# Order of the 28 products of a pair of swiglu units: by chunk pair instead of by product

## Chip, cores and metric

The kernel runs on one NeuronCore of a Trainium2 chip, in one launch. The metric is the device time in microseconds (us). Before the change it is 2767.7 us, the median of three runs (2762.27, 2767.70 and 2773.89). Everything is float32.

## The reference

Two blocks follow each other on one sequence of 256 tokens and width 1024. The first is an attention and gating layer with a mixture of 16 experts. The second is two layers (DEPTH_2 = 2), each with a swiglu, a mixer of four branches and a second swiglu. The changed code belongs to the swiglus of the second block, four in all:

```
D_MODEL = 1024; D_FF = 2816; DEPTH_2 = 2
def swiglu(x, w_gate, w_up, w_down):
    return (jax.nn.silu(x @ w_gate) * (x @ w_up)) @ w_down
for l in range(DEPTH_2):
    x = x + 0.5 * swiglu(rms_norm(x, ffn1_norm[l]), ffn1_w_gate[l], ffn1_w_up[l], ffn1_w_down[l])
    ...                                   # mixer
    x = x + 0.5 * swiglu(rms_norm(x, ffn2_norm[l]), ffn2_w_gate[l], ffn2_w_up[l], ffn2_w_down[l])
```

## The kernel before

**Weights.** SyncE loads all weights in units of 128 x 2048 float32 (1 MB) into a ring of 12 slots. A unit's load waits until the unit 12 places earlier is done, which TensorE tells through the semaphore unit_done. A swiglu stage has 11 pairs (PAIRS) of a gate unit and an up unit, each 256 columns of w_gate and w_up. Then come 11 units of w_down for the steps.

**Products.** For a pair j, both [256 tokens x 1024] x [1024 x 256] products are made together with seven products of halves instead of eight (a Strassen-like scheme). Tokens are halved into rows 0 to 127 and 128 to 255, and the contraction is halved into even and odd 128-blocks. The contraction of 1024 is eight chunks, or four chunk pairs k = 0 to 3. Product i of chunk pair k is one 128x128 by 128x256 product, and the profile shows it as two matmul instructions. So a pair has 7 x 4 = 28 products, or 56 matmuls. Their operands are the chunks of ZT (products 1, 2, 4), sums of activation chunks (3, 5, 6, 7, written by input_sums), and units of the ring or sums of weights (4, 5, 6; 7 reads a half of the up unit that VectorE has overwritten with a difference). VectorE makes the weight sums of a pair in four operations (pair_weights, L2455 to L2461, two of them as part 0 and two as part 1). Each adds one to weights_summed. GpSimd makes those of the very first pair (L2985 to L2990).

**PSUM.** Two sets of four banks alternate between pairs. In a set, product 1 has bank 3. Products 2 and 6 share bank 0, 5 and 7 share bank 1, 3 and 4 share bank 2.

**TensorE's order.** It is written out by hand. ffn runs pair 0, then pairs 1 to 10, then 22 steps for w_down (L1278). In the function pair, all four chunk pairs of product 1 come first, then those of 2, 3, 6, 7, 5 and 4. Pair 0 of the first stage of layer 0 goes through pair; the other three pair 0s go through by_chunks (from L1341), which already runs over chunk pairs and, in each, over 1, 2, 3, 6, 7, 5, 4. Before product 5 of pair j, turn_hidden (L1309 and L1316) transposes the hidden rows of pair j-1. In pair 0 of the first stage the small gain sums of final_sums (L1249, 32 matmuls of two columns) stand there instead. At its start a pair j >= 2 waits for hidden_out of pair j-2, a pair 1 of the first stage waits ahead of product 3 for mean_ready, and product 6 and product 4 wait for three and four of the weight sums.

**Behind the products.** ScalarE copies product 1 (L1940) after the first ffn_full. VectorE adds banks 0, 1 and 2 in turn (combine, L2533, L2536, L2540 and L2541), each behind the product that fills the bank. ScalarE applies silu (L1954, L1956), VectorE multiplies (L2614) into the hidden rows H, and ScalarE copies the transposed rows out (L1969, hidden_out). In pairs 1 to 4 of the first stage ScalarE has two more copies in front of that (L1964). ScalarE's program order is: silu of j, silu of j, product 1 of j+1, turned rows of j. VectorE's is: combine of j, weight sums of j+2 part 0, H of j, weight sums of j+2 part 1.

**Ahead of the first stage.** The input chunks of ZT are made by ScalarE (L1895) and VectorE (L2360), the activation sums by VectorE (L2465 to L2470).

Of the kernel before, what the change touches and what calls it, by code (L numbers as in the profile page):

```python
# [125 lines left out]
def nth_summed(l, st, i):  # L126

    n = nth_weights(l, st)
    if i == 0 and (l, st) == (0, FFN1):
        return 0  # L130
    if i == 0 and st != PROJ:
        before = (l, PROJ) if st == FFN2 else (l - 1, FFN2)
        return nth_weights(*before) + NEXT_AT[before[1]]
    return n + i + (st in NEXT_AT and (l, st) != (NL - 1, FFN2) and i >= NEXT_AT[st])
# [82 lines left out]
def build(nc, a, out, const, const_at):  # L217
    with ExitStack() as ctx:
# [84 lines left out]
        unit_done = sem("unit_done")  # L303
# [90 lines left out]
        ffn_full = sem("ffn_full")  # L394
        weights_summed = sem("weights_summed")
        acts_summed = sem("acts_summed")
        sums_used = sem("sums_used")
# [460 lines left out]
        def _(pe):  # L858
# [48 lines left out]
            def zg_chunk(v, k):  # L907

                if by_scalar(v, k):
                    pe.wait_ge(zg_out_a, chunk_out(v, k))  # L910
                else:
                    pe.wait_ge(zg_out_v, chunk_out(v, k))
# [19 lines left out]
            for b in range(4):  # L932
                for c in range(2):
                    for t in range(TT):
                        last = tr(ps[:, b, 256 * c + P * t:256 * c + P * t + P],
                                  X[:, t, P * (2 * b + c):P * (2 * b + c) + P], ident)
# [12 lines left out]
            for m, u in enumerate((0, 1, 2, 2, 3, 4, 5, 6)):  # L949
# [4 lines left out]
                for t in range(TT):  # L954
                    for k in range(KC):
                        if m in (0, 3) and t == 0:
                            pe.wait_ge((lhs_a, lhs_v)[k % 2], 4 * (m // 3) + k // 2 + 1)
                        last = mm(ps[:, 4 + m % 4, 256 * t:256 * t + 256], src[:, k, P * t:P * t + P],
                                  slot(U_WIN + u)[:, 256 * k:256 * k + 256], start=(k == 0), stop=(k == KC - 1))
# [4 lines left out]
            for n in range(2):  # L964
                for g in range(4):
                    last = tr(ps[:, n, P * g:P * g + P], wsR[:, 4 * n + g, :], ident)
                last.then_inc(turn_full, 1)
            pe.wait_ge(heads_ready, 1)
            for n in range(2):
                for c in range(2):  # L970
                    for t in range(TT):
                        last = tr(ps[:, 2 + n, 256 * c + P * t:256 * c + P * t + P],
                                  RQ1[:, t, 2 * (2 * n + c):2 * (2 * n + c) + 2, :].rearrange("p h d -> p (h d)"), ident)
# [3 lines left out]
            for g in range(2):  # L977
                for s in range(4):
                    last = tr(ps[:, g, P * s:P * s + P], KN1[:, s, g].rearrange("p u d -> p (u d)"), ident)
# [80 lines left out]
            for t in range(TT):  # L1060
                for g in range(8):
                    last = mm(ps[:, t, HD * g:HD * g + HD], wsT[:, g, :], B1[:, t, FB_VV + HD * g:FB_VV + HD * g + HD],
                              start=True, stop=True)
# [15 lines left out]
            for k in range(KC):  # L1079
                last = mm(ps[:, 7, 16:16 + NE], BB[:, k, :], slot(U_ROUTER)[:, NE * k:NE * k + NE],  # L1080
                          start=(k == 0), stop=(k == KC - 1))
            for i in range(2):
                for h in range(2):
                    last = mm(ps[64 * h:64 * h + 64, 7, 32:40].rearrange("p (j i) -> p i j", i=2)[:, i, :],
                              ident.rearrange("p (q i) -> p i q", i=2)[:, i, :],
                              scaleB[:, 2, :].rearrange("p (j h) -> p h j", h=2)[:, h, :], start=True, stop=True)
# [6 lines left out]
            for c in range(KC):  # L1093
                if c >= 4:
                    pe.wait_ge(xt_new, c - 3)
                for k in range(KC):
                    if c == 0:
                        pe.wait_ge(y_out, k // 2 + 1)
                        if k % 2 == 0:
                            wait_unit(pe, U_WOUT + k // 2)  # L1100
                    last = mm(ps[:, 4 + c % 4, 256 * (c // 4):256 * (c // 4) + 256],
                              slot(U_WOUT + k // 2)[:, D * (k % 2) + P * c:D * (k % 2) + P * c + P], ZT[:, k, :],
                              start=(k == 0), stop=(k == KC - 1))
# [6 lines left out]
            for k in range(KC):  # L1110
# [4 lines left out]
                for t in range(TT):  # L1115
                    last = mm(ps[:, 4, NE * t:NE * t + NE], RZ[:, k, P * t:P * t + P], slot(U_ROUTER)[:, NE * k:NE * k + NE],
                              start=(k == 0 and t == 0), stop=(k == KC - 1), skip_group_check=True)
# [10 lines left out]
            for t in range(TT):  # L1128
                last = tr(ps[0:NE, 5, P * t:P * t + P], AFF[:, t, :], ident)
# [106 lines left out]
            for l in range(NL):  # L1236
# [7 lines left out]
                def final_sums():  # L1244

                    for t in range(TT):
                        for k in range(KC):
                            pe.wait_ge(squares_out, KC + k + 1)
                            last = mm(ps[:, 2, 2 * t:2 * t + 2], SQ0[:, k, P * t:P * t + P], gsq[:, k, :],  # L1249
                                      start=(k == 0), stop=(k == KC - 1))  # L1250
                    last.then_inc(sums_out, 1)
# [45 lines left out]
                def ffn(st, first, v):  # L1297
# [3 lines left out]
                    def turn_hidden(j):  # L1301

                        pe.wait_ge(ffn_hidden, done + j + 1)
                        at = 4 * pair_set(st, j)
                        if v == 1 and 1 <= j < 5:
                            pe.wait_ge(fin_scaled, 1)
                            for c in range(2):
                                for t in range(TT):
                                    tr(ps[:, at + 1, 256 * c + P * t:256 * c + P * t + P],  # L1309
                                       XT[:, 2 * (j - 1) + c, P * t:P * t + P], ident)  # L1310
                        if st == FFN2 and l + 1 < NL and j == 1:
                            pe.wait_ge(v2_in, 16 * V2_LOADS * (l + 2))
                            tr(ps[:, at + 1, 0:V2_N], vrow[0:V2_N, :], ident[0:V2_N, 0:V2_N]).then_inc(cols_turned, 1)
                        for e in range(2):
                            for t in range(TT):
                                last = tr(ps[:, at, 256 * e + P * t:256 * e + P * t + P], H[:, t, P * e:P * e + P], ident)  # L1316
                        last.then_inc(rows_turned, 1)

                    def product(j, i, k, **kw):

                        n = U_LAYER + first + 2 * j
                        gate, up = slot(n), slot(n + 1)
                        even, odd = slice(512 * k, 512 * k + 256), slice(512 * k + 256, 512 * k + 512)
                        sums, wsum = z_sums(k // 2)[:, k % 2], pair_sums(j)
                        at = product_out(pair_set(st, j), i)
                        if i == 1:
                            return mm(at, ZT[:, 2 * k, 0:P], gate[:, even], **kw)  # L1327
                        if i == 2:
                            return mm(at, ZT[:, 2 * k + 1, 0:P], gate[:, odd], **kw)  # L1329
                        if i == 3:  # L1330
                            return mm(at, sums[:, 3], up[:, odd], **kw)  # L1331
                        if i == 4:
                            return mm(at, ZT[:, 2 * k + 1, P:T], wsum[:, 2, k], **kw)  # L1333
                        if i == 5:
                            return mm(at, sums[:, 0], wsum[:, 0, k], **kw)  # L1335
                        if i == 6:
                            return mm(at, sums[:, 1], wsum[:, 1, k], **kw)  # L1337
                        return mm(at, sums[:, 2], up[:, even], **kw)  # L1338
# [28 lines left out]
                    def pair(j):  # L1367

                        wait_unit(pe, U_LAYER + first + 2 * j, turns)
                        wait_unit(pe, U_LAYER + first + 2 * j + 1, turns)  # L1370
                        if j >= 2:
                            pe.wait_ge(hidden_out, done + j - 1)
                        for i in (1, 2, 3, 6, 7, 5, 4):
                            if j == 1 and i == 3 and v == 1:
                                pe.wait_ge(mean_ready, 3)
                            if i == 6:
                                pe.wait_ge(weights_summed, 4 * nth_summed(l, st, j) + 3)
                            if i == 5 and j:
                                turn_hidden(j - 1)
                            if i == 5 and j == 0:  # L1380
                                final_sums()
                            if i == 4:
                                pe.wait_ge(weights_summed, 4 * nth_summed(l, st, j) + 4)
                            for k in range(4):
                                if j == 0 and i < 3:
                                    zg_chunk(v, 2 * k + i - 1)
                                if j == 0 and i == 3 and k % 2 == 0:
                                    pe.wait_ge(acts_summed, 4 * (ns + k // 2) + 4)
                                last = product(j, i, k, start=(k == 0), stop=(k == 3))
                                if i == 4 and k < 2:  # L1390
                                    last.then_inc(unit_done, 1)
                            if i in (1, 6, 5):
                                last.then_inc(ffn_full, 1)
                        last.then_inc(sums_used, 1)

                    def before(i, b, k):

# [153 lines left out]
                for s in range(2):  # L1551
                    for hh in range(2):
                        last = mm(ps[:, 4, 64 * s + 32 * hh:64 * s + 32 * hh + 30], GB[:, s, P * hh:P * hh + P], C("stack")[:, 0:30],
                                  start=True, stop=True)
# [1491 lines left out]
```

## Time and profile before

| | us or share |
|---|---|
| Median of three runs | 2767.7 |
| The profiled execution's own time | 2772.29 |
| Its span (first to last instruction) | 2770.5 |
| TensorE matmul busy | 2551.8 (92%) |
| VectorE busy | 991.1 (36%) |
| ScalarE busy | 430.9 (16%) |
| Mean granted TensorE clock | 0.917 |
| One pair in steady state | 12.53 |

The profile is of one execution, and all rows quoted below come from it. Times in its tables count from the start of the span. The first 1145 us are the first block. The four swiglu stages start at 1150, 1758, 1967 and 2558 us. The granted clock is given as a share of full speed: 1.00 is 2.4 GHz and 0.50 is 1.2 GHz. Matmuls overlap by a little, so the spacing of their starts, not their duration, is what one costs.

### The profile page before, as it was taken

The numbers are of one execution on the slowest core, as the hardware profiler recorded it, in microseconds if no ns is written. First come the engines' busy times: TensorE is split into PE (matmuls) and PEld (weight loads), VectorE is DVE, ScalarE is ACT, GpSimd is POOL, SyncE is SP. The second block draws the span as 40 slices with busy tenths as digits, with TensorE's granted clock in tenths as the row PEclk, the third lists the DMA queues.
The fourth block names the chain that finished last, engine by engine and source line by source line (L and its number), as shares of the span: only waits on it lengthen the run. The fifth ranks groups of instructions, "written<-read, shape, count | busy, mean of one in ns | idle before, by whom it ended". The sixth has DMA issues, their size and how long they took to land.

```text
span 2770.5 us, 33932 instructions
## 1 busy us (share of the span) xinstructions
PE 2551.8 (92%) x14163; PEld 1951.3 (70%) x14163; DVE 991.1 (36%) x2011; ACT 430.9 (16%) x960; POOL 57.1 (2%) x65
## 2 busy tenths in 40 slices
PE   7998878888888878799999999999999999999999
PEld 5784434444445444588898788888888897788888
DVE  1421101010000010366523522767666325515665
ACT  2321101011011010111012420110110113401110
POOL 0000000000000000100010000000000010000000
PEclk8997877788777787799999999999999999999999
DMA  9647999999999999954565344554554555355440
GB/s 358 234 183 314 428 428 429 428 428 429 428 429 428 429 428 429 362 170 165 154 170 171 102 123 140 173 174 167 159 176 167 154 154 168 80 158 173 152 166 17
DMA packets 250735, 694.50 MB, mean 251 GB/s; under 512 B 11024, under 2 KB 193664, under 8 KB 225536
## 3 DMA queue, kind: packets, MB, share of 16 engines
q1 hardware_dynamic: 248160, 688.54, 66.6%
q10 hardware_dynamic: 2464, 4.39, 0.4%
q8 instruction: 80, 1.31, 0.2%
q14 instruction: 31, 0.25, 0.0%
HBM read 691.85 MB, written 1.05 MB: 250 GB/s over the span
## 4 chain that ended last, share of the span: by engine, by line
PE 84%; DMA 11%; DVE 2%; ACT 1%; issue 1%; POOL 0%; SPq 0%; DVEq 0%; ACTq 0%
PE banks L1278 11%; DMA ring<-in_w 11%; PE banks L1646 8%; PE banks L1182 7%; PE banks L1198 6%; PE banks L925 4%; PE banks L1729 4%; PE banks L1169 4%; PE banks L1455 3%; PE banks L1335 3%; PE banks L1331 3%; PE banks L1333 3%; PE banks L1329 3%; PE banks L1338 3%; PE banks L1337 3%; PE banks L1327 3%
## 5 line engine op out<-in xcount | busy, mean ns | idle before, releaser
L1169 PE MATMUL banks<-ring,BK 128*32 128x512 f32 x2048 | 274.4, 677 | 127.6 <-DMA ring<-in_w 115.2
L1169 PEld LDWEIGHTS banks<-ring,BK 128*32 128x32 f32 x2048 | 64.5, 117 | 321.5 <-issue 153.5
L1646 PE MATMUL banks<-ZT,ring 128*128 128x256 f32 x1024 | 232.3, 380 | 0.1
L1646 PEld LDWEIGHTS banks<-ZT,ring 128*128 128x128 f32 x1024 | 192.6, 190 | 28.8 <-issue 3.6
L1198 PE MATMUL banks<-ring,GB 128*32 128x512 f32 x976 | 150.1, 758 | 0.0
L1182 PEld LDWEIGHTS banks<-cst,PB 128*128 128x128 f32 x512 | 93.1, 280 | 44.7 <-ACT QT L1918 44.7
L1182 PE MATMUL banks<-cst,PB 128*128 128x32 f32 x512 | 95.8, 355 | 24.1 <-DVE QT L2427 24.1
L1729 PE MATMUL banks<-YT,ring 128*128 128x256 f32 x512 | 117.2, 379 | 0.0
L2427 DVE COPY QT<-banks 128x512 f32<-128x512 f32 x32 | 20.6, 686 | 262.1 <-PE banks L1169 262.1
L1182 PE MATMUL banks<-cst,QT 128*128 128x32 f32 x512 | 113.2, 396 | 0.0
L925 PE MATMUL banks<-ring,ZT 128*128 128x256 f32 (+2 forms) x576 | 112.4, 357 | 0.0
L1182 PEld LDWEIGHTS banks<-cst,QT 128*128 128x128 f32 x512 | 110.8, 327 | 0.0
L925 PEld LDWEIGHTS banks<-ring,ZT 128*128 128x128 f32 x576 | 105.5, 190 | 6.7
L1729 PEld LDWEIGHTS banks<-YT,ring 128*128 128x128 f32 x512 | 97.1, 190 | 14.7 <-issue 1.6
L2456 DVE TENSOR_TENSOR ring<-ring 128x256 f32<-128x256 f32 (+1 forms) x147 | 95.9, 653 | 0.0
L2455 DVE TENSOR_TENSOR QT<-ring 128x256 f32<-128x256 f32 (+1 forms) x124 | 68.4, 551 | 72.3 <-PE banks L1278 72.2
L1327 PE MATMUL banks<-ring,ZT 128*128 128x256 f32 x352 | 86.0, 382 | 6.5 <-ACT ZT L1895 6.1
L1278 PE MATMUL banks<-ring,PB 128*128 128x256 f32 x352 | 90.4, 379 | 0.0
L1198 PEld LDWEIGHTS banks<-ring,GB 128*32 128x32 f32 x976 | 32.2, 134 | 77.4 <-issue 75.6
L1329 PE MATMUL banks<-ring,ZT 128*128 128x256 f32 x352 | 86.4, 385 | 0.0
L2430 DVE TENSOR_TENSOR GB<-KCV,banks 128x256 f32<-128x256 f32 x32 | 13.5, 421 | 202.9 <-ACT KCV L1921 202.9
L1455 PE MATMUL banks<-ZT,ring 128*128 128x256 f32 x384 | 83.2, 379 | 0.0
(460 smaller groups left out, 4003.8 us busy)
## 6 DMA issues: line engine op xcount, KB each, us to landing
ring<-in_w SPq DMA_DIRECT2D x189, 2048.0 KB, 20.3
ring<-in_w_in SPq DMA_DIRECT2D x71, 1024.0 KB, 5.3
ring<-in_ffn_w_gate SPq DMA_DIRECT2D x44, 1024.0 KB, 5.5
ring<-in_ffn_w_up SPq DMA_DIRECT2D x44, 1024.0 KB, 7.8
ring<-in_ffn_w_down SPq DMA_DIRECT2D x44, 1024.0 KB, 5.2
ring<-in_w_mod SPq DMA_DIRECT2D x24, 1024.0 KB, 11.6
ring<-in_w_out SPq DMA_DIRECT2D x12, 1024.0 KB, 4.9
ring<-in_w_branch SPq DMA_DIRECT2D x8, 1024.0 KB, 5.9
```

Of the source, the lines that this page charges most:

```text
L925: last = mm(ps[:, bank, width * t:width * t + width], src[:, k, P * t:P * t + P], slot(n)[:, width * k:width * k + width], start=(k == 0), ...
L1169: last = mm(ps[32 * j:32 * j + 32, 4 + b, :], XE[:, k, :], slot(n)[:, 512 * b:512 * b + 512], start=(k < 4), stop=(k >= 4))
L1182: last = mm(ps[:, 4 + h, c:c + 32], cols, C("stack"), start=True, stop=True)
L1198: last = mm(ps[32 * j:32 * j + 32, 6 + half, :], HT[:, 2 * u + i, :], w[:, D * i + 512 * half:D * i + 512 * half + 512], start=(u < 2), st ...
L1278: return mm(product_out(at, j), lhs, rhs, start=(k == 0 and opens), stop=end, skip_group_check=True)
L1327: return mm(at, ZT[:, 2 * k, 0:P], gate[:, even], **kw)
L1329: return mm(at, ZT[:, 2 * k + 1, 0:P], gate[:, odd], **kw)
L1331: return mm(at, sums[:, 3], up[:, odd], **kw)
L1455: last = mm(ps[:, 4 + m % 4, 256 * c:256 * c + 256], w[:, P * c:P * c + P], ZT[:, k, :], start=(k == 0), stop=(k == KC - 1))
L1646: last = mm(out, slot(n)[:, 256 * k + P * (c % 2):256 * k + P * (c % 2) + P], ZT[:, k, :], start=(k == 0), stop=(k == KC - 1))
L1729: last = mm(ps[:, 4 + q % 4, 256:512], slot(br + k // 2)[:, D * (k % 2) + P * c:D * (k % 2) + P * c + P], YT[:, b, k, :], start=(k == 0), ...
L2456: tt(b12, b22, b12, ALU.subtract).then_inc(weights_summed, 1)
```

## The change

In the function pair the loop over chunk pairs is now the outer one, and each chunk pair runs products 1, 2, 3, 6, 7, 5, 4. All waits that stood between products now stand at the start of the pair. The transposes (or the gain sums in pair 0 of the first stage) stand ahead of the last chunk pair. The semaphores for finished products are raised by the products of the last chunk pair. by_chunks and steps are as they were. The same 28 products are issued.

```diff
-                        for i in (1, 2, 3, 6, 7, 5, 4):
-                            if j == 1 and i == 3 and v == 1:
+                        if j == 0:
+                            for i in (1, 2):
+                                for k in range(4):
+                                    zg_chunk(v, 2 * k + i - 1)
+                            pe.wait_ge(acts_summed, 4 * ns + 8)
+                        pe.wait_ge(weights_summed, 4 * nth_summed(l, st, j) + 4)
+                        for k in range(4):
+                            if k == 3:
+                                turn_hidden(j - 1) if j else final_sums()
+                            if j == 1 and k == 0 and v == 1:
                                 pe.wait_ge(mean_ready, 3)
-                            if i == 6:
-                                pe.wait_ge(weights_summed, 4 * nth_summed(l, st, j) + 3)
-                            if i == 5 and j:
-                                turn_hidden(j - 1)
-                            if i == 5 and j == 0:
-                                final_sums()
-                            if i == 4:
-                                pe.wait_ge(weights_summed, 4 * nth_summed(l, st, j) + 4)
-                            for k in range(4):
-                                if j == 0 and i < 3:
-                                    zg_chunk(v, 2 * k + i - 1)
-                                if j == 0 and i == 3 and k % 2 == 0:
-                                    pe.wait_ge(acts_summed, 4 * (ns + k // 2) + 4)
-                                last = product(j, i, k, start=(k == 0), stop=(k == 3))
-                                if i == 4 and k < 2:
-                                    last.then_inc(unit_done, 1)
-                            if i in (1, 6, 5):
-                                last.then_inc(ffn_full, 1)
-                        last.then_inc(sums_used, 1)
+                            opens, adds = dict(start=(k == 0), stop=(k == 3), skip_group_check=True), dict(
+                                start=False, stop=(k == 3), skip_group_check=True)
+                            p1 = product(j, 1, k, **opens)
+                            product(j, 2, k, **opens)
+                            p3 = product(j, 3, k, **opens)
+                            p6 = product(j, 6, k, **adds)
+                            p7 = product(j, 7, k, **opens)
+                            p5 = product(j, 5, k, **adds)
+                            p4 = product(j, 4, k, **adds)
+                        p1.then_inc(ffn_full, 1)
+                        p3.then_inc(unit_done, 1)
+                        p6.then_inc(ffn_full, 1)
+                        p7.then_inc(unit_done, 1)
+                        p5.then_inc(ffn_full, 1)
+                        p4.then_inc(sums_used, 1)
```

## Rows read from the trace of the kernel before

**Rows 1.** The page: clock by slice, and the chain that ended last, by engine.

```profile
PEclk8997877788777787799999999999999999999999
...
PE 84%; DMA 11%; DVE 2%; ACT 1%; issue 1%; POOL 0%; SPq 0%; DVEq 0%; ACTq 0%
```

**Rows 2.** Table by stretch: length, busy of each engine (count), clock, DMA share, GB/s.

```profile
1178.80:1305.80 127.00, 127.00 (x617) 112.05 (x617) 81.88 (x124) 21.88 (x48) 0.00 (x0) 1.00 0.48 166
1305.80:1373.60 67.80, 67.80 (x321) 59.74 (x321) 41.79 (x120) 4.15 (x10) 0.00 (x0) 1.00 0.56 175
...
1758.40:1764.50 6.10, 6.10 (x30) 5.31 (x29) 3.33 (x8) 1.45 (x4) 0.92 (x3) 1.00 0.59 182
...
1785.98:1898.00 112.02, 112.02 (x539) 98.67 (x538) 73.72 (x114) 17.12 (x37) 0.00 (x0) 1.00 0.50 169
```

**Rows 3.** Timeline, TensorE, two pair starts: start us, length us, engine, line, operation.

```profile
1178.83 1.89 PE L1327 MATMUL banks<-ring,ZT 128*128 128x256 f32 x8
...
1191.36 1.89 PE L1327 MATMUL banks<-ring,ZT 128*128 128x256 f32 x8
```

**Rows 4.** Timeline, start of the first swiglu stage: TensorE, GpSimd, VectorE.

```profile
1150.29 1.03 PE L1327 MATMUL banks<-ring,ZT 128*128 128x256 f32 x4
...
1152.98 2.34 POOL L2990 TENSOR_TENSOR YT<-ring,YT 128x1024 f32<-128x1024 f32 x1
...
1158.12 1.22 PE L1327 MATMUL banks<-ring,ZT 128*128 128x256 f32 x2 [5.34 <-ACT ZT L1895]
...
1159.80 0.42 DVE L2470 TENSOR_TENSOR QT<-ZT,QT 128x256 f32<-128x256 f32 x1
...
1168.47 4.63 PE L1249 MATMUL banks<-small,PB 128*128 128x2 f32 x32
```

**Rows 5.** Table by stretch, TensorE alone: length, busy (count), clock, DMA share, GB/s.

```profile
1161.00:1164.00 3.00, 3.00 (x9) 0.50 1.10 347
...
1164.00:1165.00 1.00, 1.00 (x6) 0.98 1.11 351
...
1170.00:1171.00 1.00, 1.00 (x10) 0.94 1.10 346
...
1177.00:1178.00 1.00, 1.00 (x5) 0.65 0.00 0
```

**Rows 6.** Timeline, TensorE in by_chunks, second stage: starts of two chunk pairs.

```profile
1758.46 0.59 PE L1327 MATMUL banks<-ring,ZT 128*128 128x256 f32 x2
...
1761.48 0.59 PE L1327 MATMUL banks<-ring,ZT 128*128 128x256 f32 x2
```

**Rows 7.** Timeline, VectorE and TensorE around the second stage's pair 1.

```profile
1771.55 1.23 DVE L2461 TENSOR_TENSOR QT<-ring,QT 128x1024 f32<-128x1024 f32 x1
...
1772.70 0.68 DVE L2533 TENSOR_TENSOR ZP<-ZP,banks 128x512 f32<-128x512 f32 x1
...
1773.45 1.89 PE L1327 MATMUL banks<-ring,ZT 128*128 128x256 f32 x8
...
1773.48 0.69 DVE L2536 TENSOR_TENSOR ZP<-ZP,banks 128x512 f32<-128x512 f32 x1
```

**Rows 8.** Timeline, VectorE behind the pair that ends at 1191.36.

```profile
1191.56 0.69 DVE L2540 TENSOR_TENSOR ZP<-ZP,banks 128x512 f32<-128x512 f32 x1 [1.04 <-PE banks L1333]
...
1194.77 0.88 DVE L2614 SCALAR_TENSOR_TENSOR ZP<-ZP,small 128x256 f32<-128x256 f32 x2
...
1196.81 1.23 DVE L2461 TENSOR_TENSOR QT<-ring,QT 128x1024 f32<-128x1024 f32 x1
```

**Rows 9.** Timeline, VectorE's first combination of pair 10, behind the steps' sums.

```profile
1303.91 0.68 DVE L2533 TENSOR_TENSOR ZP<-ZP,banks 128x512 f32<-128x512 f32 x1
```

**Rows 10.** Timeline, ScalarE in the first stage's pair 2: product 1, two copies, turned rows.

```profile
1193.29 0.38 ACT L1940 ACTIVATE ZP<-banks 128x256 f32<-128x256 f32 x1 [0.49 <-PE banks L1327]
1201.07 0.84 ACT L1964 ACTIVATE X<-banks,small 128x256 f32<-128x256 f32 x2 [7.40 <-PE banks L1316]
1201.80 0.60 ACT L1969 ACTIVATE PB<-banks 128x512 f32<-128x512 f32 x1
```

## The prediction

> **What bounds the kernel now.** I read the page's slices and chain first [rows 1]. The chain of what ended last is TensorE for 84% of the span and a DMA for 11%. The clock digits are 7 to 9 in the first 17 slices and 9 in all the later ones. But for its first 29 us, the changed code runs only in these later slices, in the four swiglu stages (two layers, two stages each, 11 pairs of units a stage). The table by stretch comes next [rows 2]. Pairs 1 to 10 of the first stage, the 22 steps behind them, and a later run of pairs show TensorE busy for the whole stretch (127.00 of 127.00 us, 67.80 of 67.80, 112.02 of 112.02) with a granted clock of 1.00. That is the higher of its two levels, 2.4 GHz. The list of waits has no row at all for TensorE in any of these stretches. So inside the pairs TensorE ends every wait last, and an order of products can gain nothing there but can lose.
>
> A product is two matmul instructions. In the product order a pair starts at 1178.83 and the next at 1191.36 [rows 3]. That is 12.53 us: 56 matmuls at 0.216 us (eight of one product span 1.89 us with the 0.38 of the last), and the remaining 0.43 us for four transposes. The one place with a margin either way is the start of the first stage, layer 0, from 1150.3 to 1178.8 us [rows 4, 5]. There TensorE waits for its input to be normalised and runs partly at the lower clock. It is the only pair 0 that goes through the changed function. The other three pair 0s use by_chunks, which the diff leaves alone.
>
> **Part 1: the order itself, 41 pairs.** The same 56 matmuls are issued with the same operands, and no DMA is added or moved. by_chunks already issues exactly the new order. There the seven products of one chunk take 1758.46 to 1761.48 = 3.02 us, or 0.431 us a product [rows 6], the same as 2 x 0.216 in the product order [rows 3]. Its stretch has TensorE busy 6.10 of 6.10 us at clock 1.00 [rows 2]. Cost: 0. Bounds: nothing shows a product faster than 0.431 or slower at full clock, and the modelled starts agree to about 2 ns. Over 41 x 28 products that is within 2.3 us either way.
>
> **Part 2: results come in a bunch at the end of the pair.** Call T the start of the next pair. Product 6 of the last chunk now ends at T-1.1 (seven matmuls of 0.216 before T, plus 0.38 for its own). Product 5 ends at T-0.27, and product 4 just after T as before. VectorE's first combination (0.69 us) thus starts at T-1.1, the second at T-0.25, and the third 0.79 us later (the spacing of two dependent ones when both inputs are ready, 1772.70 and 1773.48 [rows 7]), at T+0.54. Before, it starts at T+0.20 (1191.56 [rows 8]). So all of VectorE's work behind it moves 0.34 us later. That work is the hidden rows (end 1195.65, T+4.3, so T+4.6 after) and the weight sums of the pair after next (end 1198.04, T+6.7, so T+7.0). The transposes of the hidden rows sit before the last chunk, 21 products or 9.07 us behind T, which leaves 4.4 us. The weight sums are wanted at the start of the pair after next, T+12.5, which leaves 5.5 us. Both are hidden under TensorE. The fullest VectorE stretch, before pair 10 ends, is done at 1303.91 [rows 9], and the new first combination cannot start before 1304.7, so it delays nothing. Its hidden rows are turned behind two steps (6.0 us past that pair's end), against 4.6.
>
> Cost 0. If the cover were gone each pair would pay the excess, and the rival below is priced so.
>
> **Part 3: ScalarE's copies.** Transposes of pair j-1 now start at 7 x 0.432 + 0.43 = 3.46 us before the end of pair j. ScalarE is in order: it first copies product 1 (0.38 us, and only once its last chunk is done, 2.44 us before the end), then the turned rows (0.60 us), done at about 1.4 us before the end. In pairs 1 to 4 of the first stage two more copies (0.73 us between 1201.07 and 1201.80 [rows 10]) stand between, leaving 0.7 us. Before, the margin was 1.9 us there: 1201.80 + 0.60 against the next start, 1191.36 + 12.53 + 0.43 = 1204.32. The next pair, or step 0, waits for that copy at its very start. TensorE's whole queue stands behind it, and behind TensorE both the freeing of ring slots and VectorE. This is the tightest new margin. It is positive in all 40 places, so cost 0.
>
> **Part 4: all four weight sums before the first product.** Before, product 6 waited for three of them and product 4 for the last. In steady pairs they are 5.5 us early. For pair 1 of the three later stages VectorE ends them at 1771.55 + 1.23 = 1772.78, and the pair starts at 1773.45 [rows 7]. Margin 0.67 us, cost 0. All three stages show this same margin, and one stands for them. Ring slots come free at products 24 and 26 instead of 25 and 26, for loads six pairs ahead: 0.
>
> **Part 5: pair 0 of the first stage.** Before, the 16 matmuls of products 1 and 2 ran from 1150.29 on as input chunks arrived, with 5.34 us of waiting before 1158.12 [rows 4]. Now nothing starts until all eight chunks, both halves of the activation sums and the four weight sums are there. The last of these is VectorE's sum at 1159.80 + 0.42 = 1160.22 (GpSimd's last weight sum ends at 1155.32). So TensorE starts at 1160.3 with 42 matmuls ahead of the gain sums, instead of 40 of which 6 were done early. The clock is at the lower level (0.50, 1.2 GHz) after the idle stretch and until 1164.0 [rows 5]. A matmul takes twice 0.216, so 0.43 us, at that level. Lower bound: the clock rises at the same instant, so 3.7 us low = 8.7 matmuls, and 33.3 x 0.216 = 7.2 us, giving 1171.2. Upper bound: it rises as long after the first matmul as before (5.9 us from 1158.12), so 13.8 low and 28.2 high = 6.1, giving 1172.3. Against 1168.47 that is +2.7 to +3.8.
>
> Behind it one product fewer is left, 0.43 us saved, so +2.3 to +3.4 if the 32 small matmuls of the gain sums and the rest run as before (10.36 us to 1178.83). In that stretch the clock fell to 0.50 from 1170.9 and came back at 1177.7 [rows 5]. All at the high level would be about 32 x 0.1 (ten in the 1 us row at 0.94) + 14 x 0.216 = 6.2 us, or 4.1 less than 10.4. At the low level a small one takes at most 0.28 us (seven in the last 2.0 of their 4.5 us, if 25 went at 0.1), so all there would be 32 x 0.28 + 14 x 0.427 = 15.0, or 4.6 more. So the bounds of the part are -1.4 (2.7 - 4.1) and +8.4 (3.8 + 4.6), and the same pattern as before is nearest. I take +2.5, since the lower start bound asks for nothing new. The wait for the mean moves to pair 1's start, but VectorE makes it in two operations on two columns straight behind the gain sums, with 14 matmuls (3.0 us or more) still to go: 0. Nothing later absorbs the shift, because all behind it is paced by TensorE.
>
> **Sum.** 0 + 0 + 0 + 0 + 2.5 = +2.5 us, or 2772.3 + 2.5 = 2774.8 on the profiled execution's own time (span 2770.5 and 1.8 around it). The median of three runs is 2767.7, 4.6 below that, inside their own spread of 11.6. On that scale the forecast is 2770.2.
>
> **Rivals.** (a) Slower by ScalarE's late copy: the 0.7 to 1.4 us margins of part 3 are worked out, not seen. If the path from product 1's end to the hidden rows' copy is longer than the rows' durations add up to, each of 40 pairs stalls by the excess. From 1.75 us of path beyond my sum (0.35 us a pair) it decides: +14 us. With 2.1 us beyond, 0.7 x 40 = +28 us, 2798. For it speaks only that TensorE's queue has no slack elsewhere. Against it, ScalarE's copy of product 1 starts at 1193.29, 0.04 us after the end of that product (1191.36 + 1.89), so the release itself is quick [rows 3, 10].
>
> (b) The cycling over four banks with both operands new each time costs clock. Its place is all 41 pairs: 10% of their 12.1 us at the low level would cost 41 x 0.6 = +25 us, 2795. Against it, the same order in by_chunks and the near-same one in the steps hold clock 1.00 over 67.80 us [rows 2]. The Trainium skill has such a rule (TensorE: Matmul & The Clock Gate, "A second HAM failure mode: psum-queue depth-cycling"): cycling through PSUM banks gives micro-idles in which the clock oscillates. By that rule the time would be (b)'s. The trace disagrees at 1.00.
>
> (c) Faster: the clock. With TensorE idle to 1160.3 and then dense, the low phase around the gain sums goes away, -1.4 us by the bound above. To pass -14 us it would need a gain inside pairs that are already 127.00 of 127.00 busy. About 2766 if it holds.
>
> (d) The new order changes something the model of the trace hides, such as sequencer time per accumulation switch, 12 ns a product. 1148 x 12 ns = 14 us, 2784 or 2754. The 0.431 above speaks against it.
>
> **How the numbers follow.** A measurement of this kernel can tell about 0.5% (13.8 us) from no change. The forecast with part 5 anywhere in its bounds has 0.80, (a) 0.05, (b) 0.03, (c) 0.07 and (d) 0.05. Faster by over 0.5%: half of (d) and a little of (c), 0.04. Slower: (a), (b) and a part of (d), 0.09. Within: 0.87. The range starts at 2762, 1.4 under the median with 4 for the spread of runs. It ends at 2783, part 5's upper bound (2776) with the spread and into (d).
>
> **What would show it.** In the changed trace, the first matmul of the first pair comes at 1160.3, behind VectorE's sum and no longer behind ScalarE's chunk. Pair 1 starts at 1181.3 (1178.9 to 1183 still fits). Pair starts are 12.53 us apart with no TensorE wait, VectorE's third combination comes at T+0.54, and ScalarE's copy of turned rows ends 1.4 us before T. It is wrong if pairs are longer than 12.6 us, if TensorE waits for a ScalarE copy at L1372, or if the clock in the pairs is under 1.00.

## The result and the profile after

The changed kernel takes 2772.39 us (median of 12 runs, 2767.97 to 2778.24) against 2767.26 us for the kernel before on the same chip (12 runs, 2762.27 to 2773.89). The ratio is 1.0021, 95% interval 1.0013 to 1.0030: 5.1 us slower by the medians. That is more than its measurement is uncertain, and well inside the 0.5% that the prediction calls no change. The time forecast was 2770.2 us in a range of 2762 to 2783.

The profiled execution of the changed kernel has a span of 2768.0 us, less than the 2770.5 us of the one before. A single pair of profiles thus gives the wrong sign. TensorE's clock accounts for most of that. In the layer-0 mixer, which the change does not touch, the kernel before happened to run at 0.55 for 5 us and the changed one did not. The table by stretch (length, busy of each engine with its count, clock, DMA share, GB/s) shows it, for the kernel before first and then for the changed one:

```profile
1530.00:1535.00 5.00, 4.54 (x50) 4.21 (x47) 3.63 (x13) 0.61 (x1) 0.19 (x1) 0.77 1.01 373
1535.00:1540.00 5.00, 5.00 (x26) 4.72 (x27) 0.39 (x1) 1.75 (x5) 0.00 (x0) 0.55 0.12 34
```

```profile
1530.00:1535.00 5.00, 4.53 (x66) 4.13 (x63) 4.06 (x14) 1.34 (x2) 0.72 (x2) 1.00 0.95 338
1535.00:1540.00 5.00, 5.00 (x36) 4.29 (x35) 2.43 (x5) 2.65 (x11) 0.00 (x0) 1.00 0.27 84
```

The same 24 matmuls of one line there took 5.49 us before and 2.94 us after, 2.55 us less:

```profile
1533.72 5.49 PE L1598 MATMUL banks<-PB,ZP 128*128 128x128 f32 x24
```

```profile
1534.09 2.94 PE L1602 MATMUL banks<-PB,ZP 128*128 128x128 f32 x24
```

So the sizes below are read from the stretch that changed and from many runs, not from the spans.

**The pairs.** The table by stretch of the changed kernel for pairs 1 to 10 of the first stage, the steps behind them, and the later run of pairs, answering to [rows 2]:

```profile
1179.60:1306.60 127.00, 127.00 (x618) 112.05 (x617) 81.94 (x125) 21.86 (x49) 0.00 (x0) 1.00 0.48 166
1306.60:1374.40 67.80, 67.80 (x322) 59.75 (x321) 42.17 (x121) 4.34 (x11) 0.00 (x0) 1.00 0.55 174
...
1786.80:1898.80 112.00, 112.00 (x539) 98.65 (x538) 73.30 (x116) 17.15 (x37) 0.00 (x0) 1.00 0.49 167
```

Length, busy time and clock are as before. The timeline of the changed kernel's pair 1 and the start of pair 2 (TensorE first, then VectorE, then ScalarE, and last ScalarE's copy in pair 2 and TensorE's start of pair 3; start, length, engine, line), answering to [rows 3, 8 and 10]:

```profile
1179.57 0.59 PE L1327 MATMUL banks<-ring,ZT 128*128 128x256 f32 x2
1180.00 0.59 PE L1329 MATMUL banks<-ring,ZT 128*128 128x256 f32 x2
...
1188.63 0.60 PE L1316 MATMUL banks<-cst,ZP 128*128 128x128 f32 x4
...
1192.10 0.59 PE L1327 MATMUL banks<-ring,ZT 128*128 128x256 f32 x2
...
1191.07 0.69 DVE L2537 TENSOR_TENSOR ZP<-ZP,banks 128x512 f32<-128x512 f32 x1 [4.46 <-PE banks L1337]
1191.86 0.69 DVE L2540 TENSOR_TENSOR ZP<-ZP,banks 128x512 f32<-128x512 f32 x1
1192.65 0.69 DVE L2544 TENSOR_TENSOR ZP<-ZP,banks 128x512 f32<-128x512 f32 x1
...
1189.70 0.38 ACT L1944 ACTIVATE ZP<-banks 128x256 f32<-128x256 f32 x1 [8.35 <-PE banks L1327]
1189.99 0.59 ACT L1973 ACTIVATE PB<-banks 128x512 f32<-128x512 f32 x1
...
1203.66 0.61 ACT L1973 ACTIVATE PB<-banks 128x512 f32<-128x512 f32 x1
...
1205.06 0.59 PE L1327 MATMUL banks<-ring,ZT 128*128 128x256 f32 x2
```

The pair takes 1192.10 - 1179.57 = 12.53 us, and a product 0.43. With T = 1192.10, VectorE's three combinations start at T-1.03, T-0.24 and T+0.55 (forecast T-1.1, T-0.25, T+0.54). ScalarE's copy of the turned rows ends at 1190.58, T-1.5 (forecast T-1.4). In pair 2, with its two extra copies, it ends at 1204.27, 0.8 us before the next pair (forecast 0.7). TensorE has no wait at all from 1179.6 to 1374 us. The margin of the second stage's pair 1 is 0.67 us, as in [rows 7]:

```profile
1769.21 1.23 DVE L2465 TENSOR_TENSOR QT<-ring,QT 128x1024 f32<-128x1024 f32 x1
...
1771.11 0.59 PE L1327 MATMUL banks<-ring,ZT 128*128 128x256 f32 x2
```

**The first pair.** The timeline of the changed kernel, answering to [rows 4]:

```profile
1146.91 3.69 PE L1223 MATMUL banks<-BK,PB 128*128 128x256 f32 x16 [0.88 <-ACT PB L1927]
1159.94 1.19 PE L1327 MATMUL banks<-ring,ZT 128*128 128x256 f32 x2 [9.34 <-DVE QT L2474]
...
1171.30 3.74 PE L1249 MATMUL banks<-small,PB 128*128 128x2 f32 x32
```

The first product waits 9.34 us for VectorE's last activation sum (L2474, formerly L2470), no longer for ScalarE's chunk.

The last work ahead of it (L1223, the last expert's scatter) gives every profile of this stretch the same zero. Before, one execution was profiled; the experiments gave two more of each kind (times in us from the start of L1223, each from the profile's timeline):

| first pair | profile | dense products from | gain sums at | pair 1 at |
|---|---|---|---|---|
| old | kernel before | 11.35 | 21.70 | 32.06 |
| old | again (e11) | 11.41 | 20.53 | 29.24 |
| old | e1 | 11.20 | 20.17 | 28.89 |
| new | changed kernel | 13.03 | 24.39 | 32.66 |
| new | again (e12) | 13.20 | 24.55 | 32.82 |
| new | e2 | 13.42 | 24.60 | 32.87 |

The means of the last column are 30.06 and 32.78, a difference of 2.7 us. The medians are 29.24 and 32.82, a difference of 3.6.

The old pair's spread is 3.2 us, and its dense products start within 0.2 us in all three. The rest is when the clock rises and falls. From the start of the dense products on, TensorE worked at 0.50 for about 12.7 us in the kernel before, and for 6.8 and 6.5 us in e11 and e1. In the three new pairs it was 7.9, 7.9 and 7.6 us. Half of that time is what the lower level cost: 6.4, 3.4 and 3.3 us in the old pairs, 3.9 on average in the new ones. These are estimates from the granted clock of each microsecond.

So the profiles name what the new pair loses. It starts 1.9 us later, and the six matmuls that the old pair had done before its last wait now come behind the wait, 6 x 0.216 = 1.3 us. Together that is 3.2. The lower level adds about half a us to this against e11 and e1, and takes about half a us off against the mean of all three.

### The profile page after: what moved, and what is told of

It is laid out like the page before. It is cut to its first block, busy times and chain, and to the rows that moved or that the text cites. A ratio compares the mean times of both kernels' runs of the same rounds, so it can differ in the third digit from the quotient of the medians.

```text
span 2768.0 us, 33974 instructions
## 1 busy us (share of the span) xinstructions
PE 2545.6 (92%) x14163; PEld 1948.6 (70%) x14163; DVE 990.5 (36%) x2011; ACT 431.0 (16%) x960; POOL 57.1 (2%) x65
## 4 chain that ended last, share of the span: by engine, by line
PE 84%; DMA 11%; DVE 2%; ACT 1%; issue 1%; POOL 0%; SPq 0%; DVEq 0%
PE banks L1278 11%; DMA ring<-in_w 11%; PE banks L1650 8%; PE banks L1182 7%; PE banks L1198 6%; PE banks L925 4%; PE banks L1733 4%; PE banks L1169 4%; PE banks L1459 3%; PE banks L1331 3%; PE banks L1337 3%; PE banks L1338 3%; PE banks L1327 3%; PE banks L1333 3%; PE banks L1335 3%; PE banks L1329 3%
## 5 line engine op out<-in xcount | busy, mean ns | idle before, releaser
L1650 PE MATMUL banks<-ZT,ring 128*128 128x256 f32 x1024 | 232.3, 380 | 0.1
L1327 PE MATMUL banks<-ring,ZT 128*128 128x256 f32 x352 | 106.3, 384 | 9.7 <-DVE QT L2474 9.3
L1944 ACT ACTIVATE ZP<-banks 128x256 f32<-128x256 f32 x56 | 21.5, 384 | 593.1 <-PE banks L1327 367.4
L1329 PE MATMUL banks<-ring,ZT 128*128 128x256 f32 x352 | 105.6, 382 | 0.0
L2537 DVE TENSOR_TENSOR ZP<-ZP,banks 128x512 f32<-128x512 f32 x56 | 38.5, 687 | 174.5 <-PE banks L1337 166.4
```

The costliest lines, as they stand in the source:

```text
L1650: last = mm(out, slot(n)[:, 256 * k + P * (c % 2):256 * k + P * (c % 2) + P], ZT[:, k, :], start=(k == 0), stop=(k == KC - 1))
```

## Experiments

Each ran beside runs of the kernel before on the same chip. A change in us is the difference of the two medians. The ratio is given with its 95% interval. It is not the quotient of these medians and can differ from it: in e6 the ratio of 0.9990 would be 2.8 us, the medians are 1.0 us apart. Line numbers differ between kernels: L1371 or L1370 are inserted operations.

**e1: the 40 later pairs alone.** Only pair 0 of the first stage keeps the old function, here called pair_first:

```diff
-                    by_chunks() if v > 1 else pair(0)
+                    by_chunks() if v > 1 else pair_first(0)
```

> Pair 0 of the first stage in the old product order with its waits between the products, all 40 other pairs in the chunk order. Theory A (the whole change of about +5 us sits in pair 0 of the first stage, where the work that TensorE did while input chunks arrived is given up and the lower clock hits what follows): ratio to the kernel before 1.0000, within 0.001. Theory B (the 40 later pairs cost 0.13 us each, in a way that one profile does not show): 1.0018 to 1.0021.

Measured: 2765.28 against 2765.46 us, ratio 1.0002 (0.9993 to 1.0011), -0.2 us by the medians. Theory A. The chunk order of 40 pairs costs nothing that can be measured, and its interval does not reach theory B's 1.0018.

**e2: pair 0 of the first stage alone.** The mirror of e1: pair_first has the new body, pair the old one.

> Pair 0 of the first stage as in the changed kernel (all waits ahead of the first product, chunk order), the 40 other pairs in the old order. Theory A: ratio 1.0018 to 1.0021, that is +5 to +6 us. Theory B: 1.0000, within 0.001.

Measured: 2771.04 against 2765.46 us, ratio 1.0019 (1.0009 to 1.0028), +5.6 us. The whole cost is here.

**e3: only the waits of pair 0 moved.** The order of products stays the old one:

```diff
+                        if j == 0:
+                            for i in (1, 2):
+                                for k in range(4):
+                                    zg_chunk(v, 2 * k + i - 1)
+                            pe.wait_ge(acts_summed, 4 * ns + 8)
+                            pe.wait_ge(weights_summed, 4 * nth_summed(l, st, j) + 4)
                         for i in (1, 2, 3, 6, 7, 5, 4):
```

> The kernel before, with one thing changed: in pair 0 of the first stage all waits stand ahead of the first product. The order of products is the old one. Theory A1 (the early waits cost): ratio 1.0015 to 1.0025, the same as with the new order. Theory A2 (the order of products and the place of the gain sums in pair 0 cost, not the waits): 1.000 to 1.0005. Theory B: 1.0000.

Measured: 2769.39 against 2765.46 us, ratio 1.0011 (1.0002 to 1.0020), +3.9 us. That is under the expected 1.0015 to 1.0025 of theory A1, whose range its interval reaches, and over the 1.0005 of A2, which its interval reaches too. So the times alone do not choose between the two. They exclude theory B's 1.0000, and by the medians the waits are most of the cost. The 1.7 us between e3 and e2 are inside their intervals, so whether the order adds anything in pair 0 is open from the times. By the profile it adds nothing: e3's stretch is 32.99 us with the old order, as long as the new pair 0's 32.66 to 32.87. e4 asks the same from the other side.

**e4: chunk order with each wait at its product.** In pair 0 of the changed kernel:

```diff
-                        if j == 0:
-                            for i in (1, 2):
-                                for k in range(4):
-                                    zg_chunk(v, 2 * k + i - 1)
-                            pe.wait_ge(acts_summed, 4 * ns + 8)
-                        pe.wait_ge(weights_summed, 4 * nth_summed(l, st, j) + 4)
...
+                            zg_chunk(v, 2 * k)
                             p1 = product(j, 1, k, **opens)
+                            zg_chunk(v, 2 * k + 1)
                             product(j, 2, k, **opens)
+                            pe.wait_ge(acts_summed, 4 * (ns + k // 2) + 4)
                             p3 = product(j, 3, k, **opens)
+                            pe.wait_ge(weights_summed, 4 * nth_summed(l, st, j) + 4)
                             p6 = product(j, 6, k, **adds)
```

> The changed kernel, but pair 0 of the first stage waits for each input chunk and each half of the activation sums just before the product that reads it. Theory A1: most of the cost comes back; TensorE runs dense from the first half of the activation sums (about 1156.7 us) instead of 1160.3, so ratio 0.999 to 1.0005. Theory A2: stays at 1.002. Theory B: 1.0018 to 1.0021.

Measured: 2766.87 against 2765.46 us, ratio 1.0001 (0.9992 to 1.0010), +1.4 us by the medians. The cost is gone as far as the runs can tell, with the chunk order everywhere, and the stretch is 28.53 us. So the order is not the cause in pair 0 either. The waits in front of the loop are. The timeline of this kernel shows two products done early and the dense work beginning 10.16 us after L1223, against 13.0 to 13.4 with the waits in front:

```profile
1149.82 3.69 PE L1223 MATMUL banks<-BK,PB 128*128 128x256 f32 x16 [0.87 <-ACT PB L1958]
1153.34 0.60 PE L1327 MATMUL banks<-ring,ZT 128*128 128x256 f32 x2
1153.93 0.70 PE L1329 MATMUL banks<-ring,ZT 128*128 128x256 f32 x2
1159.98 1.22 PE L1331 MATMUL banks<-ring,YT 128*128 128x256 f32 x2 [5.34 <-DVE YT L2505]
```

The next four ask what the lower clock costs in either pair. Extra products of a constant by a constant keep TensorE at work in a wait. Their result is overwritten by the first real product in that bank.

**e5: the changed kernel, its wait filled.**

```diff
+                    def fill(n):
+                        for _ in range(n):
+                            mm(ps[:, 6, 0:256], ident, C("iota"), start=True, stop=True)
...
                         if j == 0:
+                            fill(21)
```

> The changed kernel with 21 extra products of a constant by a constant (42 matmuls, 9.07 us at 0.216) in the 9.3 to 9.7 us in which TensorE waits ahead of the first pair; their result is overwritten. Theory clock (a good part of the cost is the lower clock after the empty stretch: some 3.5 to 6 us at half speed): the granted clock is 1.00 at the first product, the gain sums start 9.1 us after it instead of 11.2, ratio to the kernel before 1.000 to 1.0012, so 2 to 4 us under the changed kernel. Theory work (the cost is only the 16 matmuls given up and the later start, the clock being low in the kernel before as well): ratio stays at 1.0018 to 1.0021.

Measured: 2767.84 against 2765.54 us, ratio 1.0006 (0.9998 to 1.0015), +2.3 us. By the medians some 3 us come back with nothing but dummy work. The interval just overlaps that of the changed kernel (1.0013 to 1.0030), so the size is rough. The timeline shows the mechanism: products start at full clock, and the gain sums follow 9.07 us later instead of 11.36. The stretch is 29.93 us, 2.9 under the new pair's mean. This is what the lower level costs the new pair. It is no share of what the change added, because the old pair pays it too (e8).

```profile
1151.13 9.23 PE L1370 MATMUL banks<-cst 128*128 128x256 f32 x42
1160.19 0.59 PE L1327 MATMUL banks<-ring,ZT 128*128 128x256 f32 x2
...
1169.26 3.86 PE L1249 MATMUL banks<-small,PB 128*128 128x2 f32 x32
```

**e6: the kernel before, gain sums spread.** final_sums is cut into its 16 products, two of them behind each chunk product of products 6 and 7:

```diff
-                            if i == 5 and j == 0:
-                                final_sums()
...
+                                if j == 0 and i in (6, 7):
+                                    for n in range(2):
+                                        gain_sum((i - 6) * 8 + 2 * k + n)
```

> The kernel before with the 32 small matmuls of the gain sums spread in fours behind each of the eight chunk products of products 6 and 7 of pair 0, instead of in one block ahead of product 5. If the block is what lets the clock fall (0.50 from 1170.9 to 1177.7 in the kernel before), the clock stays 1.00 through the pair and 2 to 4 us go: ratio 0.9985 to 0.9995. If it falls for another reason, 1.0000 within 0.0005.

Measured: 2764.57 against 2765.54 us, ratio 0.9990 (0.9982 to 0.9999), -1.0 us by the medians. In its profile the clock stays at 1.00 from 1164 us on, and the stretch is 28.73 us, only 0.2 to 0.5 us under e1's and e11's. The clock does what was expected, but the gain is at the edge of what the runs can tell.

**e7: the kernel before, its wait filled.** fill(12) ahead of the wait for the fourth chunk of product 1.

> The kernel before with 12 extra products (24 matmuls, 5.2 us) of a constant by a constant in its own 5.34 us wait of pair 0. Theory clock: the half-speed stretch behind the wait goes (1 to 6 us long, so 0.5 to 3 us gained), ratio 0.9988 to 0.9998. Theory work: 1.0000 or a little above, if the extra products run into the awaited chunk.

Measured: 2765.44 against 2765.54 us, ratio 0.9995 (0.9986 to 1.0004), -0.1 us by the medians. The ratio is inside the expected range, but its interval holds 1: no gain that can be told. The profile (stretch 29.15 us) says where it may have gone. The first products run at 1.00, but the clock then falls within the block of gain sums and stays low for 6.8 us, as in the profile of the kernel before and twice as long as in e11 and e1:

```profile
1166.00:1168.00 2.00, 2.00 (x20) 1.00 1.10 349
1168.00:1170.00 2.00, 2.00 (x14) 0.60 1.13 354
1170.00:1172.00 2.00, 2.00 (x8) 0.50 0.66 218
1172.00:1174.00 2.00, 2.00 (x7) 0.50 0.11 39
1174.00:1176.00 2.00, 2.00 (x8) 0.70 0.00 0
```

**e8: both of the last two.**

> The kernel before with both the extra products in the wait and the gain sums spread. Clock 1.00 from 1150 on to the end of pair 0; ratio 0.9980 to 0.9992 (3 to 5 us under the kernel before) by theory clock, 1.0000 by theory work.

Measured: 2763.23 against 2765.54 us, ratio 0.9989 (0.9980 to 0.9998), -2.3 us. In its profile the clock is 1.00 throughout and the stretch 26.29 us, 3.8 under the old pair's mean and the shortest with GpSimd's sums in place. By these profiles the lower level costs the old pair about as much as the new one. This kernel beats both, by a little. Its profile may flatter it: of the 12 runs six lie from 2758.9 to 2761.9 us and six from 2764.6 to 2767.6, and the profiled one (2760.22) is among the six short ones.

**e9: the first pair's weight sums on VectorE**, in the kernel before. The four operations on GpSimd are deleted, and VectorE does them behind the second half of the activation sums:

```diff
-            nc.gpsimd.tensor_tensor(first_sums[:, 0], up[:, :, 0], gate[:, :, 0], ALU.subtract).then_inc(weights_summed, 1)
...
+                    for part in range(2):
+                        weight_sums(0, [pair_sums(0)[:, i] for i in range(3)], gate[:, :, 0], up[:, :, 0], gate[:, :, 1], up[:, :, 1], part)
                     tt(XT, XT, over(gfin, T), ALU.mult).then_inc(fin_scaled, 1)
```

> The kernel before with the four weight sums of the very first pair moved from GpSimd (2.35 us each, 1145.9 to 1155.3) to VectorE, behind the activation sums. Theory: while GpSimd runs, three of VectorE's operations take 1.53, 1.65 and 2.44 us where they take 0.34, 0.34 and 0.42 otherwise; that goes, the last input chunk comes 4.5 us earlier (about 1153.6) and the last activation sum at about 1155.7; the weight sums end near 1160.3, the third of them is awaited by product 6 at about 1159.4 instead of 1165.0. Ratio 0.9980 to 0.9990 (3 to 5.5 us less). Rival: the slowness of these operations is not GpSimd's, and the four sums on VectorE come late: ratio 1.0000 to 1.002.

Measured: 2759.33 against 2766.80 us (8 and 20 runs), ratio 0.9972 (0.9962 to 0.9982), -7.5 us. This is the fastest kernel of the study: 0.28% under the kernel before, where the changed kernel is 0.21% over it. VectorE's timeline around the activation sums, in the kernel before and then in e9:

```profile
1151.40 1.65 DVE L2360 TENSOR_SCALAR ZT<-X,small 128x256 f32<-128x256 f32 x1
1153.16 2.44 DVE L2465 TENSOR_TENSOR YT<-ZT 128x256 f32<-128x256 f32 x1
1155.53 0.41 DVE L2466 TENSOR_TENSOR YT<-ZT 128x256 f32<-128x256 f32 x1
```

```profile
1150.63 0.34 DVE L2389 TENSOR_SCALAR ZT<-X,small 128x256 f32<-128x256 f32 x1
1151.08 0.42 DVE L2494 TENSOR_TENSOR YT<-ZT 128x256 f32<-128x256 f32 x1
1151.42 0.42 DVE L2495 TENSOR_TENSOR YT<-ZT 128x256 f32<-128x256 f32 x1
```

The operations that took 1.65 and 2.44 us beside GpSimd's take 0.34 and 0.42. The Trainium skill (SBUF — State Buffer, "Who interferes with whom") has this rule: a VectorE operation with two SBUF inputs is blocked by a GpSimd operation that reads SBUF, for the whole of it. The trace agrees. By that rule the first two-input sum waits for the GpSimd sum that holds the port, which ends at 1155.32 [rows 4], and the next one starts at 1155.53. That the operations with one input, among them the one of 1.65 us, are short again without GpSimd's sums is shown by this run alone. TensorE's last wait for a chunk shrinks from 5.34 to 1.76 us:

```profile
1147.18 3.69 PE L1223 MATMUL banks<-BK,PB 128*128 128x256 f32 x16 [0.87 <-ACT PB L1952]
1150.71 1.54 PE L1327 MATMUL banks<-ring,ZT 128*128 128x256 f32 x6
1154.02 0.70 PE L1327 MATMUL banks<-ring,ZT 128*128 128x256 f32 x2 [1.76 <-ACT ZT L1924]
...
1159.58 1.13 PE L1337 MATMUL banks<-YT 128*128 128x256 f32 x4 [1.42 <-DVE YT L2488]
...
1170.17 1.89 PE L1327 MATMUL banks<-ring,ZT 128*128 128x256 f32 x8
```

The stretch is 22.99 us, 7.1 under the old pair's mean, which accounts for nearly all of the 7.5 us. That is more than the expected 3 to 5.5 us. In this profile the clock is also at 1.00 from 1150 us to the end of the pair, where the old pairs lost 3.3 to 6.4 us to the lower level. That the shorter wait is the reason was not tested apart.

**e10: e9 with e6's spread.**

> e9 with the gain sums spread behind products 6 and 7 as in e6. If the two gains add: ratio 0.9970 to 0.9982. If the earlier start already keeps the clock from falling at the gain sums, the same as e9.

Measured: 2763.68 against 2766.80 us, ratio 0.9984 (0.9975 to 0.9994), -3.1 us. Neither expectation holds: it is slower than e9 by 4.4 us by the medians, with intervals that overlap a little. Its profile names a cost that e6's did not show. The clock fell in the middle of the spread gain sums and stayed low for most of 13 us, with the same two waits of TensorE ahead of it (1.76 and 1.42 us) as in e9:

```profile
1161.00:1174.00 13.00, 13.00 (x47) 0.52 1.10 348
```

The stretch is 29.63 us, 6.6 more than e9's. It need not fall so each time. Five of e10's 12 runs lie from 2757.1 to 2758.9 us, as short as e9's, and seven from 2763.2 to 2768.3, on average 6.8 us longer. The profiled run (2765.91) is one of the seven. That the five are those in which the clock held was not seen.

**e11 and e12: the two kernels once more, for a second profile.**

> The kernel before, for a second profile of the first pair. From the last expert's scatter (L1223) to the start of pair 1 it took 32.06 us in the first profile and 28.89 with the same pair 0 in e1. If the phase of the clock changes is random, anything from 28.5 to 32.5; the clock in the wait and at the gain sums tells which.

> The changed kernel, for a second profile of the first pair. The same stretch took 32.66 and 32.87 us in two profiles of the new pair 0. Anything from 32 to 36 if the clock's phase is random.

Measured: 2766.89 and 2768.18 us, one run each. The profiles give the stretches of the table above, 29.24 and 32.82 us. The clock in the two, first e11 and then e12 (length, busy with count, clock, DMA share, GB/s):

```profile
1158.00:1160.00 2.00, 1.15 (x3) 0.50 1.10 350
1160.00:1162.00 2.00, 2.00 (x7) 0.50 1.10 347
1162.00:1164.00 2.00, 2.00 (x10) 0.93 1.10 349
1172.00:1174.00 2.00, 2.00 (x8) 0.63 1.10 347
1174.00:1176.00 2.00, 2.00 (x6) 0.52 0.44 142
```

```profile
1158.00:1160.00 2.00, 1.67 (x4) 0.50 1.10 347
1160.00:1162.00 2.00, 2.00 (x6) 0.50 1.11 349
1162.00:1164.00 2.00, 2.00 (x9) 0.80 1.10 348
1172.00:1174.00 2.00, 2.00 (x14) 0.76 0.13 38
1174.00:1176.00 2.00, 2.00 (x7) 0.50 0.00 0
```

## Why the prediction was right, and where its sizes were off

**Parts 1 to 4 (cost 0).** Right, each at its size. Pairs of 12.53 us, no TensorE wait, combinations within 0.07 us of the forecast times, ScalarE's copy within about 0.1 us. e1 confirms it by the runs: 1.0002. Rivals (a), (b) and (d) fall with it. (b) was the Trainium skill's rule on cycling through PSUM banks, and 127.00 of 127.00 us at clock 1.00 under the new order shows none of it.

**Part 5 (+2.5).** The place is right, shown by e2. The mechanism is right, with its two sides: the start moves from ScalarE's chunk to VectorE's last sum (forecast 1160.3, found 1159.94), and the gain sums come at 1171.3, the lower bound of 1171.2. The clock rose within half a us of where it did before. The rest behind them took 8.27 us where "the same pattern as before" gave 9.93, that is 10.36 less one product of 0.43. It was that pattern that was unusual: e11 and e1 have 8.71 and 8.72 us there, or 8.28 and 8.29 less the product. Pair 1 came at 1179.57, inside the stated 1178.9 to 1183.

**What was mis-sized** is the term +2.5 itself, by the runs: +5.1 and, in e2, +5.6, twice as much. It was worked out against one execution of the kernel before, whose first pair was an unlucky one: 32.06 us where two other profiles have 29.24 and 28.89. That the term is near the 2.7 us between the means of the profiles is partly luck. The prediction put pair 1 34.5 us behind L1223, 1.7 us later than the new pair's mean, and its starting point was 2.0 us over the old pair's mean. The two errors nearly cancel. The range of 21 us was wide enough for either size.

**What the +5.1 is made of.** That it sits in the waits of the first pair is shown (e2, e3, e4). Of its size, the later start and the six matmuls that are no longer done early explain 3.2 us. The lower clock, which the prediction rightly let act on both kernels, is no large part of the difference in the profiles: between half a us more and half a us less. With the clock held up, the stretch shrinks by 2.9 us in the new pair (e5) and by 3.8 in the old one (e8). What stays open is the 2.4 us between the 2.7 of three profiles a side and the 5.1 of the runs (1.5 by the profiles' medians). The interval of the runs begins at 3.6 us. The clock's phase differs in each execution and three profiles are few, but that it fills the gap was not shown.

Rival (c)'s own claim, that a dense start makes the low stretch at the gain sums go away, is refuted. The clock fell in the three profiles of the new pair, and in e5 too, although there TensorE had been busy at 1.00 for 18 us before the gain sums.

## What to carry to other kernels

A wait moved in front of a loop is free where its data is always there first, in 40 of 41 places here. In the one place where data trickles in, it gives up the work done meanwhile and starts the rest later. TensorE's lower clock behind such a wait is a cost of its own: here the old order paid it too. Keep fine waits where a stage starts, and look first at what makes the data trickle. Here an idle engine's "free" help (GpSimd) slowed the one that everyone waited for, and taking it away was worth more than the whole change cost. Before pricing a difference of a few us from a single profile, check that the clock's low stretches in it are typical. The same holds for a profile of an experiment: look where the profiled run lies among all the runs.

## What the runs showed of the hardware

- GpSimd's 2.35 us sums beside VectorE raised one 0.42 us two-input operation to 2.44 us and one-input ones from 0.34 to 1.53 and 1.65 us.
- During or right behind a block of 32 matmuls of two columns, 3.6 to 4.8 us long, the granted clock fell to 0.50 in every profile of the old and the new first pair and in e3, e4, e5 and e7, for 3.4 to 6.8 us. In e9 it did not. Spread in fours between full products, the same matmuls left it at 1.00 in e6 and e8, but not in e10.
- The default is the lower level and activity lifts it, says the Trainium skill (TensorE: Matmul & The Clock Gate, "What's actually happening"). The trace agrees: 0.50 in the empty wait of both kernels, 1.00 in the same wait filled with constants (e5, e7, e8). But it also fell where the rows count TensorE busy throughout (e7 from 1168 us, e10 from 1161). When it changes is another matter: the same old first pair took 28.89, 29.24 and 32.06 us in three profiles.
